# First panel behind each norm as a plain float32 product, and one root of a doubled norm moved behind it

## What is computed

```
h = layer_norm(ALPHA * h + attention(h) @ w_out)          # per layer
h = layer_norm(ALPHA * h + relu(h @ w_up) ** 2 @ w_down)
...
xn = rms_norm(h, l0_attn_norm)                            # second block begins
proj = xn @ w_in                                          # five panels of 512 columns, and 48 gate columns
```

## Time and profile before

| | us |
|---|---|
| median of 3 runs | 2334.42 |
| lowest and highest run | 2328.5 and 2335.71 |
| the profiled execution | 2330.26 |
| its span, first to last instruction | 2328.7 |
| TensorE busy in the span | 2070.3 (89%) |
| VectorE busy | 1425.1 (61%) |
| ScalarE busy | 872.8 (37%) |

### The profile page before, as it was taken

The page is one execution under the profiler, slowest core; times in us unless marked ns, Lnnn a source line. Parts: engine busy times, 40 slices in busy tenths (PEclk is TensorE's granted clock), DMA queues, the critical chain, the costliest instruction groups (busy, mean ns, idle before and its releaser), DMA issues.

```text
span 2328.7 us, 24190 instructions
## 1 busy us (share of the span) xinstructions
PE 2070.3 (89%) x7378; PEld 1196.2 (51%) x7378; DVE 1425.1 (61%) x2980; ACT 872.8 (37%) x2116; POOL 1009.5 (43%) x1086
## 2 busy tenths in 40 slices
PE   7989999899999988898978998886999898778776
PEld 6768877778868643453424443342446344222222
DVE  3584455564477579774577654476846558684445
ACT  3645444645444432652223252223325222222222
POOL 0100000100000057677467566556746756777774
PEclk9999999999999999899999999998999999999999
DMA  8435545155535779899999999999999999999997
GB/s 309 178 115 175 193 156 205 60 178 188 184 136 183 294 319 409 345 400 412 414 410 410 416 411 412 411 414 394 403 415 408 412 412 393 410 409 409 409 409 306
DMA packets 172558, 752.66 MB, mean 323 GB/s; under 512 B 19184, under 2 KB 19472, under 8 KB 152864
## 3 DMA queue, kind: packets, MB, share of 16 engines
q0 software_dynamic: 148640, 544.05, 58.9%
q1 hardware_dynamic: 22224, 198.37, 22.5%
q10 hardware_dynamic: 1584, 8.91, 1.0%
HBM read 750.18 MB, written 4.22 MB: 324 GB/s over the span
## 4 chain that ended last, share of the span: by engine, by line
PE 46%; DMA 20%; DVE 14%; POOL 9%; issue 8%; ACT 2%; DVEq 1%; SPq 0%; ACTq 0%; POOLq 0%
PE ps L998 11%; DMA Z<-u,experts 9%; DMA Z<-v,experts 8%; PE ps L730 8%; PE ps L732 8%; PE ps L731 8%; DVE Z L2047 6%; PE ps L1018 5%; POOL Z L2411 5%; POOL Z L2426 3%; DMA ring<-v,experts 1%; POOL ring L2426 1%; DMA ring<-panels 1%; PE ps L1075 1%; DVE ring_lo L1858 1%
## 5 line engine op out<-in xcount | busy, mean ns | idle before, releaser
L998 PE MATMUL ps<-Z 128*128 128x512 f32 x1792 | 850.4, 621 | 157.2 <-DMA Z<-v,experts 96.5
L2047 DVE CUSTOM_DVE_ANT_0 Z<-Z,ps 128x1024 f32<-128x1024 f32 x512 | 611.8, 1219 | 406.6 <-DMA Z<-u,experts 400.7
L998 PEld LDWEIGHTS ps<-Z 128*128 128x128 f32 x1792 | 336.2, 197 | 630.0 <-issue 392.1
L2411 POOL DMA_INDIRECT Z<-u,experts x512 | 490.0, 957 | 286.7 <-issue 137.1
L2426 POOL DMA_INDIRECT Z<-v,experts x448 | 429.2, 958 | 254.7 <-PE ps L998 144.7
L1858 DVE TENSOR_TENSOR ring_lo<-ring,ring_hi 128x1024 fp32r<-128x1024 f32 x212 | 247.9, 1221 | 195.4 <-ACT ring_hi L1311 195.1
L1471 ACT ACTIVATE hdot<-hdot 128x4 f32<-128x4 f32 x128 | 26.3, 205 | 651.9 <-DVE hdot L2047 651.8
L730 PE MATMUL ps<-ring_hi,xT_lo 128*128 128x512 f32 x592 | 237.9, 402 | 15.9 <-DVE xT_lo L1917 9.3
L1018 PE MATMUL ps<-ring,o 128*128 128x512 f32 x528 | 232.3, 593 | 1.4 <-ACT o L1499 1.4
L731 PE MATMUL ps<-ring_lo,xT 128*128 128x512 f32 x592 | 232.6, 393 | 0.0
L732 PE MATMUL ps<-ring_hi,xT 128*128 128x512 f32 x592 | 232.5, 393 | 0.0
(11 more groups left out here) (285 smaller groups left out, 2148.6 us busy)
## 6 DMA issues: line engine op xcount, KB each, us to landing
ring<-panels SPq DMA_DIRECT2D x106, 1024.0 KB, 4.9
ring<-panels SPq DMA_DIRECT2D x37, 2048.0 KB, 10.4
Z<-u,experts POOLq DMA_INDIRECT x512, 12.7
Z<-v,experts POOLq DMA_INDIRECT x448, 13.2
Z<-panels SPq DMA_DIRECT2D x3, 2048.0 KB, 21.4
gain<-gains ACTq DMA_DIRECT2D x4, 1024.0 KB, 5.9
bias_lines<-bias_line POOLq DMA_DIRECT2D x1, 3072.0 KB, 14.2
gain<-gains ACTq DMA_DIRECT2D x5, 512.0 KB, 6.8
```

Of the source, the lines that this page charges most:

```text
L998: last = mm(ps[:, c, :], diag[s], vrow[s][:, c * NC:(c + 1) * NC], start=slot == 0, stop=slot == SLOTS - 1 or n == SUMMED[-1] - 1)
L2047: v.tensor_tensor_reduce(out=row, in0=row, in1=dotted, scale=1.0, scalar=0.0, op0=ALU.mult, op1=ALU.add, accum_out=hdot[:, t, slot:slot + 1])\
L2411: g.indirect_dma_start(out=urow[s], out_offset=None, in_=(u0, u1)[layer], in_offset=bass.IndirectOffsetOnAxis(ap=experts[:, t, slot:slot + ...
```

## The change

Behind the four turns that follow a layer norm (first MLP, second input projection, second MLP, and now the projection behind the doubled norm, whose turn becomes skewed) the first panel is no longer split. ScalarE copies the turned tokens whole to `xT_all`, and TensorE multiplies them with the panel as it landed, one float32 matmul for a piece (`whole`, `unsplit`). `xT` and `xT_lo` for the panels that follow are made from that copy: a rounding of one whole tile on ScalarE (`rounded`) and a subtraction on VectorE (`lows_of_whole`). Neither `ring_hi` nor `ring_lo` of the first panel is made; `split_place` counts the panels that are split. TensorE transposes the first half of tile 1 between two pieces of tile 0's product (before piece 6, or 7 at the doubled norm) and its second half after it; the dummy matmuls there go.

At the doubled norm xn becomes h times gain, without the root. The sum of squares is taken as before, but both tiles' roots are made together (`rms_roots`) after tile 1's normalisation. They go into the copies of the projection's results (a scale for each token) and into the gate's exponentials, which become one instruction for each tile.

The diff, without the new semaphore, the counts in the waits of split panels and the number of roots that ScalarE takes:

```
@@ -305,7 +305,13 @@
 NORMED = [{"norm": SCHEDULE[n - 1][1], "heads": "heads"}.get(SCHEDULE[n - 1][0]) for n in TURNS]
-SKEWED = [norm is not None and norm[1] == ["ln"] for norm in NORMED]
+SKEWED = [norm not in (None, "heads") for norm in NORMED]
+UNSPLIT = [FIRST[name] for name, skewed in zip(NEXT, SKEWED) if skewed]
+
+
+def split_place(first, rel):
+
+    return first + rel - sum(m <= first for m in UNSPLIT)
 
...
@@ -694,13 +701,13 @@
 
-            def transposed(turn, t):
+            def transposed(turn, t, halves=range(2)):
 
                 src = {"h": h, "xn": xn, "o": o}[TURNED[turn]]
                 if turn == 0:
                     pe.wait_ge(tokens_landed[t], 16)
                     pe.wait_ge(ident_landed, 16)
-                for kt in range(KT):
+                for kt in (4 * b + k for b in halves for k in range(4)):
                     if NORMED[turn] and kt % 4 == 0:
@@ -713,6 +720,35 @@
 
+            def turned_whole(t, k):
+
+                if k % 4 == 0:
+                    pe.wait_ge(xt_all_ready, 2 * TILES * sum(SKEWED[:turns]) + 2 * t + k // 4 + 1)
+
+            def whole(n, t, to, between):
+
+                slot = n % 2
+                for k in range(KT):
+                    if t == 0 and k % 4 == 0:
+                        pe.wait_ge(landed[slot][k // 4], 16 * (n // 2 + 1))
+                    between(k)
+                    turned_whole(t, k)
+                    last = mm(to, xT_all[:, k, t * P:(t + 1) * P], ring[:, slot, k * NC:(k + 1) * NC],
+                              start=k == 0, stop=k == KT - 1)
+                    if t == 1 and k % 4 == 3:
+                        last.then_inc(panel_used, 1)
+                return last
+
+            def unsplit(n, banks, done):
+
+                def turn_next(k):
+                    if k == (7 if len(NORMED[turns][1]) > 1 else 6):
+                        transposed(turns, 1, [0])
+
+                whole(n, 0, banks[0], turn_next).then_inc(done, 1)
+                transposed(turns, 1, [1])
+                whole(n, 1, banks[1], lambda k: None)
+
             def idle(n, to=7):
@@ -721,7 +757,7 @@
                 if NORMED[turns]:
-                    idle(4 if TURNED[turns] == "xn" else 2)
+                    idle(2)
                 transposed(turns, 1)
@@ -764,7 +800,12 @@
 
-                one(0, 0, True)
+                if SKEWED[turns]:
+                    pe.wait_ge(proj_read, 2 * done + 2)
+                    unsplit(first, [ps[:, t, :] for t in range(TILES)], proj_ready)
+                    pe.wait_ge(xt_ready, 2 * TILES * (turns + 1))
+                else:
+                    one(0, 0, True)
                 if first == FIRST["in0"]:
...
@@ -930,8 +967,9 @@
 
-                up(0, leads=True)
+                unsplit(first, [ps[:, 4 + t, :] for t in range(TILES)], up_done)
                 turn_hidden(0)
+                pe.wait_ge(xt_ready, 2 * TILES * (turns + 1))
                 up(1)
...
@@ -1323,7 +1361,30 @@
                 first, norm = FIRST[NEXT[call]], NORMED[call]
-                early = {None: 1, "heads": 3}.get(norm if norm is None else norm if norm == "heads" else 0, 2)
+                early = 3 if norm == "heads" else 1
+
+                def wholes(t):
+                    for b in range(2):
+                        act.wait_ge(xt_done, 2 * TILES * call + 2 * t + b + 1)
+                        copy(xT_all[:, 4 * b:4 * b + 4, t * P:(t + 1) * P],
+                             ps[:, 4 + 2 * t + b, :].rearrange("p (a b) -> p a b", a=4)).then_inc(xt_all_ready, 1)
+
+                def rounded(t):
+                    act.drain()
+                    copy(xT[:, :, t * P:(t + 1) * P], xT_all[:, :, t * P:(t + 1) * P]).then_inc(xt_hi, 2)
+
+                if SKEWED[call]:
+                    wholes(0)
+                    if norm[0] == "proj":
+                        evict_out(FIRST[NEXT[call]] - 2, 1, 1)
+                    rounded(0)
+                    norm_root(1, 1)
+                    wholes(1)
+                    rounded(1)
+                    if NEXT[call] == "nsa":
+                        norm_root(2, TILES)
+                        act.wait_ge(rms_ready, 1)
+                    return
 
@@ -1333,22 +1394,10 @@
                 copies(0)
-                if SKEWED[call] and norm[0] == "proj":
-                    evict_out(FIRST[NEXT[call]] - 2, 1, 1)
                 upper(first, 0, steps=range(early, CHUNKS))
                 if TURNED[call] == "o":
                     upper(first, 1)
-                if norm not in (None, "heads"):
-                    for _ in norm[1]:
-                        norm_root(1, 1)
                 copies(1)
-                if NEXT[call] == "nsa":
-                    act.wait_ge(xt_ready, 2 * TILES * (call + 1))
-                    for t in range(TILES):
-                        for b in range(2):
-                            last = copy(xT_all[:, 4 * b:4 * b + 4, t * P:(t + 1) * P],
-                                        ps[:, 4 + 2 * t + b, :].rearrange("p (a b) -> p a b", a=4))
-                    last.then_inc(xt_all_ready, 1)
 
@@ -1364,8 +1413,11 @@
                             apart(act, (panel_used, i * 4 + (2 * (first + u + 1))))
-                        copy(pj[:, t, bass.ds(i * (2 * NC) + u * NC, NC)],
-                             ps[:, 2 * u + t, :]).then_inc(proj_read, 1)
+                        to = pj[:, t, bass.ds(i * (2 * NC) + u * NC, NC)]
+                        if first == FIRST["nsa"]:
+                            f(to, ps[:, 2 * u + t, :], ACT.Copy, scale=stat[:, 2 + t:3 + t]).then_inc(proj_read, 1)
+                        else:
+                            copy(to, ps[:, 2 * u + t, :]).then_inc(proj_read, 1)
 
@@ -1564,7 +1616,9 @@
                 act.wait_ge(gate_logits, 1)
-                f(gates[:, :, :], ps[:, 4:6, 0:3 * HEADS], ACT.Exp, scale=-1.0).then_inc(gate_exps_ready, 1)
+                for t in range(TILES):
+                    last = f(gates[:, t, :], ps[:, 4 + t, 0:3 * HEADS], ACT.Exp, scale=stat[:, 58 + t:59 + t])
+                last.then_inc(gate_exps_ready, 1)
                 for tick, names in plan:
...
@@ -1762,20 +1815,22 @@
                         last.then_inc(normed, 1)
-                if kinds == ["ln"]:
-                    return
-                dve.drain()
-                v.tensor_tensor_reduce(out=o[:, t, :], in0=h[:, t, :], in1=h[:, t, :], scale=1.0, scalar=0.0,
-                                       op0=ALU.mult, op1=ALU.add, accum_out=stat[:, t:t + 1])
-                dve.drain()
-                v.tensor_scalar(stat[:, 16 + t:17 + t], stat[:, t:t + 1], 1.0 / D, RMS_EPS, ALU.mult, ALU.add)\
+                        continue
+                    dve.drain()
+                    await_gain(norm + 1)
+                    v.tensor_tensor(xn[:, t, at], h[:, t, at], gain[:, (norm + 1) % 2, at], ALU.mult).then_inc(normed, 1)
+                if kinds != ["ln"]:
+                    dve.drain()
+                    v.tensor_tensor_reduce(out=hb.rearrange("p t d -> p (t d)"), in0=h[:, t, :], in1=h[:, t, :], scale=1.0,
+                                           scalar=0.0, op0=ALU.mult, op1=ALU.add, accum_out=stat[:, 2 + t:3 + t])
+
+            def rms_roots():
+
+                dve.drain()
+                v.tensor_scalar(stat[:, 18:18 + TILES], stat[:, 2:2 + TILES], 1.0 / D, RMS_EPS, ALU.mult, ALU.add)\
                     .then_inc(squares_ready, 1)
-                inverse_roots(t, 1)
-                await_gain(norm + 1)
-                for half in range(2):
-                    at = slice(half * NC, (half + 1) * NC)
-                    v.scalar_tensor_tensor(out=xn[:, t, at], in0=h[:, t, at], scalar=stat[:, t:t + 1],
-                                           in1=gain[:, (norm + 1) % 2, at], op0=ALU.mult, op1=ALU.mult).then_inc(normed, 1)
+                inverse_roots(2, TILES)
+                v.tensor_scalar(stat[:, 58:58 + TILES], stat[:, 2:2 + TILES], -1.0, None, ALU.mult).then_inc(rms_ready, 1)
 
...
@@ -1918,15 +1973,22 @@
 
+                def lows_of_whole(t):
+                    dve.wait_ge(xt_hi, 2 * TILES * call + 2 * t + 2)
+                    cols = slice(t * P, (t + 1) * P)
+                    v.tensor_tensor(xT_lo[:, :, cols], xT_all[:, :, cols], xT[:, :, cols].bitcast(F32),
+                                    ALU.subtract).then_inc(xt_ready, 2)
+
                 name, norm = NEXT[call], NORMED[call]
-                if norm not in (None, "heads"):
-                    lower(name, 0, steps=[0, 1])
-                    lows(0)
-                    lower(name, 0, steps=[2])
+                if SKEWED[call]:
                     residual(norm[0], 1, 1)
                     variance(1)
-                    lower(name, 0, steps=[3])
                     normalize(1, norms, norm[1])
+                    lows_of_whole(0)
+                    if len(norm[1]) > 1:
+                        rms_roots()
+                    lows_of_whole(1)
```

(21 more changed lines are left out.)

## The result

The changed kernel takes **2319.32 us**, the median of four runs (2315.64 to 2320.77); the kernel before 2332.16 of four (2328.5 to 2335.71). The ratio is 0.9945, 95% interval 0.9931 to 0.9958. That is 13 us less, where 2318 was forecast. The profiled execution took 2315.64 with a span of 2314.0, against 2330.26 and 2328.7 before.

A forecast was written before the change was run, and what follows sets the result against it. TensorE, busy 89% of the span, was taken as what everything waits for in the first third. 3.0 + 4.6 + 3.0 + 11.0 = 21.6 us, less 7.2 for clock falls, left 14.4: forecast 2318 us, own range 2313 to 2323.

The forecast's parts named there:

- The price of a plain piece: Plain float32 product of a 128x512 panel piece at the joints: 0.43 us, against 0.684 for the three split matmuls.
- A: Joint where the normalised hidden state is turned and meets the first MLP's first panel: 3.0 us won.
- B: Joint at the second input projection: next panel's matmuls start at 358.2 instead of 362.89, 4.6 us won.
- C: Joint at the second MLP, the same as A shifted by 324.6 us: 3.0 us won.
- The five falls of the clock: TensorE's clock falls behind the five longest idle stretches at the joints, 1.45 us each: 7.2 us taken back.
- D: Joint at the projection behind the doubled norm: next panel starts at 685.8 instead of 696.83, 11.0 us won.
- The first, the clock holds: Rival: no clock fall lands on the path at the joints, 21.6 us stays won; 2309 to 2312, chance 0.14.
- The second: Rival: all idle stretches but the 1.35 bring clock falls, A and C give nothing; 2321 to 2325, chance 0.16.
- third: Rival: no measurable change, D's crossing costs 4 us more and clock falls everywhere; 2326 to 2330, chance 0.12.
- fourth: Rival: each of seven longer clock falls lasts into the panel behind, the kernel loses; 2340 and more, chance 0.05.
- the plain pieces at 0.9: Sign of a wrong forecast: plain pieces at the four joints spaced 0.9 us instead of 0.43.
- the gathers' stretch growing by what the front won: Sign of a wrong forecast: the last two thirds, paced by gathers of expert rows, lengthen by the time won ahead.

The follow-up runs named there:

- two_dummies: Changed kernel with two plain float32 dummy matmuls behind the first piece of the second tile at each of the four joints; 2325.24 us, ratio 0.9975.
- half_filled: half_columns with dummy matmuls in TensorE's idle stretches at the joints; 2316.78 us, ratio 0.9932.
- half_columns: Changed kernel with the plain product of the four first panels done for columns 0 to 255 of 512 only; 2318.43 us, ratio 0.995.
- tile1_split: Changed kernel with tile 1's first panel split again at the two MLPs, and squares ahead of lows at the doubled norm; 2315.84, then 2316.88 us.
- after_again: The changed kernel run once more, unaltered, beside other runs; 2319.41 us, ratio 0.9939 to the kernel before.
- abc_only: Changed kernel with the old code kept at the doubled norm, the change only at the three other joints; 2329.82 and 2329.18 us.
- root_in_chain: Changed kernel with the doubled norm's second root taken before the turn, as before the change; 2323.92 us, ratio 0.996.

## Why the forecast of the time held, and which steps failed

**The price of a plain piece failed.** The step "16 such matmuls take 6.87 us, 0.43 us each" counted rows of the chain as instructions; they were eight pieces of 0.86. The 128 rows of L736 for 64 pieces and the four rows for two dummies show it. The rule that was weighed and rejected there agrees with the trace: the Trainium skill, "FP8 and Floating Point Precision", TensorE Precision Notes, has true float32 take four passes, and 0.86 over 0.228 is 3.8. The estimate made by it, some 14 us at the joints, is what the trace has: 14.5.

**With it went A, B and C:** forecast 3.0, 4.6 and 3.0, measured 1.4, 1.8 and 1.4. TensorE became the last to arrive, which two_dummies confirms (1.7 of 1.72 us on the path at each), and with the forecast's price and a clock that holds they come out at 3.3, 4.8 and 3.3 (half_filled). The clock has no part in the small gains: at A, B and C it is 1.00 in the profile of before as in those of the changed kernel.

**The five falls of the clock failed with the same price.** 7.2 us were to be taken back; nothing was. The plain pieces, twice as long, fill the idle stretches: 0.57 instead of 3.1 in A, none in B. half_columns, where the price is the forecast's, has five falls. There the first at A and at C cost 1.6 each (16.89 and 16.97 against the 15.33 of half_filled), near the 1.45 that was put in. Those behind A and C cost more: from the hidden turn to B's and D's start it takes 172.3 and 161.0 us, against 169.1 and 158.4 in the changed kernel, 3.2 and 2.6. The one at D cost nothing (30.16 with and without it). That is 9.0 us where 7.2 was forecast.

**So two errors cancelled.** 21.6 - 7.2 = 14.4 was forecast, 14.5 + 0 happened at the joints. Both errors come from the one price, but that they are of the same size is luck. half_columns, with the forecast's price, has 21.3 - 9.0 = 12.3 in its trace and takes 2318 too. That the time fell into the forecast's own range shows the sum right and not its terms.

**D held**, the largest term: 9.9 of 11.0, and 30.16 us long with pieces at half the price too (half_columns). All its steps stand in the forecast order. Two small waits make up the 1.1: VectorE's 0.47 ahead of 667.50, in tile 1's norm, that no releaser ends, and ScalarE's start at 678.01, 0.72 behind the last small step of the roots (677.12 + 0.17), where it was put at once (ScalarE issues the load of a gain in between). The product with the gain took 0.69 (0.68 was taken between 0.61 and 0.71). The copies with a scale took 0.69 and not the 0.60 that was assumed.

**The rivals.** The first, the clock holds, was right about the clock; the joints did not give its 21.6 but 14.5. The second, third and fourth did not come. The sign named for a wrong forecast, "the plain pieces at 0.9", is the one that appeared; the other, the gathers' stretch growing by what the front won, is the point left open above.

## What to carry to other kernels

Before a duration is divided by a count of rows, count the instructions in the code: one float32 matmul was two rows here, and the price was off by a factor of two. A loop of known length in the same trace (`idle(2)`, four rows) settles it. Where a product waits for a chain of other engines, a dearer one can cost nothing, and can keep the clock up as well; find where it becomes the last to arrive, and pay for the cheaper form only there (tile1_split). When the forecast time comes out, still check the terms: an experiment at the assumed price showed two errors of 7 to 9 us with opposite signs.

## What the runs showed of the hardware

- A plain float32 matmul of 128x128 by 128x512 took 0.86 us, two rows of 0.43, and by 128x256 0.43 (six from 153.82 to 156.41 in half_filled). A float32r one takes 0.228: the split in three, 0.684, is the cheaper.
- In the first 750 us of the profiles, the length of an idle stretch of TensorE did not decide alone whether the granted clock fell to 0.50 (1.2 GHz) behind it. Behind 3.12, 3.13, 3.21, 3.90, 4.12 and 4.23 it fell. Behind 1.86, 1.88 and 2.08 (at 50 to 51 us in half_filled, after_again and two_dummies), 2.37 (the turn of D in before and in abc_only) and 2.73 it fell too. Behind 1.81, 2.01, 2.21, 2.28 (at 51 us in the first profile of the changed kernel) and 3.02 (root_in_chain, 1.00 throughout from 676 to 692) it did not.
- It can differ between executions of one kernel. An idle stretch of 2.74 us near 121 us, ahead of all joints, stands in every profile; in the first profile of the changed kernel the clock fell to 0.50 behind it, in after_again it stayed at 1.00 (TensorE of the first, then of the second: five rows in 4.11 us, six in 2.84).

```profile
121.21 4.11 PE L756 MATMUL ps<-cst,zero 128*128 128x512 f32 x5 [2.74 <-DVEq L586]
...
121.53 2.84 PE L756 MATMUL ps<-cst,zero 128*128 128x512 f32 x6 [2.74 <-DVEq L586]
```

- The clock can stay down for some 6 us: in half_columns the 128x512 matmuls from 172.03 to 175.87 are spaced 0.43 in place of 0.228, behind a turn at 169.84 that was slow already.
